# Two norms with their sums on all rows, and a sigmoid made of exponential and reciprocal, in a two-block transformer kernel

## What is computed

```python
def rms_norm(x, g):
    xf = x.astype(jnp.float32)
    y = xf * lax.rsqrt(jnp.mean(xf * xf, axis=-1, keepdims=True) + EPS)
    return (y * g.astype(jnp.float32)).astype(x.dtype)
...
        h = h + rms_norm(mixed, norm_gains[layer, 1])
        ...
        h = h + rms_norm(ffn, norm_gains[layer, 3])
    return h[:, N_META:]
...
    h = h * norm_g.astype(jnp.float32).reshape(MLSTM_HEADS, MLSTM_HEAD_DIM)
    h = h.reshape(B, S, MLSTM_WIDTH) * jax.nn.sigmoid(o_pre.astype(jnp.float32))
```

## Time and profile before

| | |
|---|---|
| median of 3 runs | 1566.23 us (1563.57 to 1566.26) |
| profiled execution | 1566.23 us, its span 1564.4 us |
| TensorE busy | 1520.0 us, 97% of the span |
| VectorE busy | 1025.5 us, 66% |
| ScalarE busy | 655.5 us, 42% |
| GpSimd busy | 21.9 us, 1% |
| DMA | 147.61 MB, mean 94 GB/s |

### The profile page before, as it was taken

The page is one execution under the profiler, slowest core; times in us unless marked ns, Lnnn a source line. Parts: engine busy times, 40 slices in busy tenths (PEclk is TensorE's granted clock), DMA queues, the critical chain, the costliest instruction groups (busy, mean ns, idle before and its releaser), DMA issues. The chain is left out here.

```text
span 1564.4 us, 25875 instructions
## 1 busy us (share of the span) xinstructions
PE 1520.0 (97%) x10760; PEld 1351.7 (86%) x10760; DVE 1025.5 (66%) x1441; ACT 655.5 (42%) x1052; POOL 21.9 (1%) x20
## 2 busy tenths in 40 slices
PE   7999999999998999999999899999999999999998
PEld 7988878888998999999888677767677999998876
DVE  5533445785446887777656666676687888885453
ACT  5433442433334222122343545545645555554343
POOL 0000000000000000000000002000000000000000
PEclk9999999999999999999999999999999999999999
DMA  5221104452331233232445213110013232222322
GB/s 180 82 82 58 38 15 155 136 165 88 106 108 68 102 129 107 102 135 75 135 134 176 94 48 102 61 35 28 28 54 108 81 109 107 97 97 83 95 90 81
DMA packets 37699, 147.61 MB, mean 94 GB/s; under 512 B 4304, under 2 KB 4432, under 8 KB 27856
## 3 DMA queue, kind: packets, MB, share of 16 engines
q1 hardware_dynamic: 36288, 142.76, 27.6%
q10 hardware_dynamic: 1152, 2.16, 0.4%
q0 software_dynamic: 144, 1.05, 0.2%
HBM read 143.86 MB, written 2.10 MB: 93 GB/s over the span
## 5 line engine op out<-in xcount | busy, mean ns | idle before, releaser
L567 PE MATMUL ps<-t 128*128 128x258 f32 (+4 forms) x2160 | 689.6, 319 | 23.7 <-DVE t L2298 8.7
L569 PE MATMUL ps<-t 128*128 128x258 f32 (+4 forms) x2160 | 678.3, 314 | 0.0
L568 PE MATMUL ps<-t 128*128 128x258 f32 (+4 forms) x2160 | 677.4, 314 | 0.0
L567 PEld LDWEIGHTS ps<-t 128*128 128x128 f32 (+1 forms) x2160 | 408.8, 189 | 67.7 <-issue 16.9
L569 PEld LDWEIGHTS ps<-t 128*128 128x128 f32 (+1 forms) x2160 | 408.5, 189 | 27.1
L568 PEld LDWEIGHTS ps<-t 128*128 128x128 f32 (+1 forms) x2160 | 409.4, 190 | 23.7
L2250 DVE TENSOR_TENSOR t<-t 128x1024 fp32r<-128x1024 f32 (+2 forms) x121 | 205.8, 1700 | 204.9 <-ACT t L1525 204.9
L1525 ACT ACTIVATE t<-t 128x1024 fp32r<-128x1024 f32 (+2 forms) x121 | 174.0, 1438 | 187.0 <-PE ps L569 175.0
L1474 PE MATMUL ps<-t 128*128 128x256 f32 x504 | 142.6, 283 | 0.0
L1472 PE MATMUL ps<-t 128*128 128x256 f32 x504 | 142.5, 283 | 0.1
L1473 PE MATMUL ps<-t 128*128 128x256 f32 x504 | 141.3, 280 | 0.0
(11 more groups left out here) (328 smaller groups left out, 1832.4 us busy)
## 6 DMA issues: line engine op xcount, KB each, us to landing
t<-in_W SPq DMA_DIRECT2D x75, 1024.0 KB, 4.8
t<-in_W SPq DMA_DIRECT2D x62, 512.0 KB, 3.6
t<-in_W SPq DMA_DIRECT2D x100, 256.0 KB, 3.8
t<-in_W SPq DMA_DIRECT2D x4, 644.0 KB, 3.8
t<-in_XT ACTq DMA_DIRECT2D x8, 264.0 KB, 7.7
out<-t SPq DMA_DIRECT2D x8, 256.0 KB, 2.5
t<-in_ROPE POOLq DMA_DIRECT2D x1, 1024.0 KB, 5.3
t<-in_CONS SPq DMA_DIRECT2D x1, 423.0 KB, 11.2
```

The lines of the kernel that those rows point to most:

```text
L567: pe.matmul(out, wh, xh, start=first, stop=False)
L568: pe.matmul(out, wh, xl, start=False, stop=False)
L569: return pe.matmul(out, wl, xh, start=False, stop=last)
```

## The change

Three things are changed.

1. Norms 1 and 3 sum over the rows by products whose left side is all ones (over 1024) on 128 rows and columns, and whose right side is the squares themselves, 512 columns wide (and 4 more for norm 1). The sums then stand on all 128 rows at once. The root is taken from there into `rst`, the reciprocal by VectorE in `rst`, and `norm_spread` and `spread` are gone for these two.
2. The gate tiles are evacuated as exp(-x), and VectorE adds 1 and takes the reciprocal, one tile at the end of each of the units 3 to 6, in place of a plain evacuation, the tanh in unit 15 and the scalings in unit 16.
3. Semaphore counts follow (`pow` and `spr` go up by two where a norm's turn was dropped).

```diff
+            def norm_total(i, b):
+
+                n, ones = NORM_N[i], C("o1024").to_broadcast([P, P])
+                for src, last in ((norm_acc(i), False), (sq[1][:, 0:n], True)):
+                    if last:
+                        pe.wait_ge(S["sq"], 8 * i + 8)
+                    else:
+                        pe.wait_ge(S["sum"], SUM0[i + 1])
+                    ins = pe.matmul(bank(b, 512), ones, src[:, 0:512], start=not last, stop=last)
+                    if n > 512:
+                        ins = pe.matmul(bank(b + 1, n - 512), ones, src[:, 512:n], start=not last, stop=last)
+                    ins.then_inc(S["col"], 1)
...
-            norm_sums(1, 4)
-            norm_sum_of(1, 4, 7)
-            norm_spread(1, 4)
+            norm_total(1, 4)
...
-            norm_sums(3, 0)
-            norm_sum_of(3, 0, 7)
-            norm_spread(3, 0)
+            norm_total(3, 0)
...
             def root(i, b):
-                ac.activation(rcol[:, 0:nc_], bank(b, nc_), ACT.Sqrt, bias=con[:, a:z]).then_inc(S["eps"], 1)
+                ac.activation(rst[:, 0:NORM_N[i]], bank(b, NORM_N[i]), ACT.Sqrt, bias=con[:, a:z]).then_inc(S["eps"], 1)
...
             root(1, 4)
-            spread(1, 4)
...
             root(3, 0)
-            spread(3, 0)
...
-            dv.reciprocal(rcol[:, 0:5], rcol[:, 0:5]).then_inc(S["pow"], 1)
+            dv.reciprocal(rst[:, 0:TQ], rst[:, 0:TQ]).then_inc(S["rst"], 1)
...
-            dv.reciprocal(rcol[:, 0:4], rcol[:, 0:4]).then_inc(S["pow"], 1)
+            dv.reciprocal(rst[:, 0:T2], rst[:, 0:T2]).then_inc(S["rst"], 1)
...
-                    ac.activation(sig[:, f - 1, :], bank(f % 2, T2), ACT.Copy).then_inc(S["ev_o2"], 1)
+                    ac.activation(sig[:, f - 1, :], bank(f % 2, T2), ACT.Exp, scale=-1.0).then_inc(S["ev_o2"], 1)
...
-                    for k in range(4):
-                        ac.wait_ge(S["ev_o2"], k + 1)
-                        ac.activation(sig[:, k, :], sig[:, k, :], ACT.Tanh, scale=0.5).then_inc(S["o2_s"], 1)
...
-                    dv.wait_ge(S["o2_s"], 4)
-                    for k in range(4):
-                        dv.tensor_scalar(sig[:, k, :], sig[:, k, :], 0.5, 0.5, ALU.mult, ALU.add).then_inc(S["o2_s"], 1)
...
+                if 3 <= u <= 6:
+                    e = sig[:, u - 3, :]
+                    dv.wait_ge(S["ev_o2"], u - 2)
+                    dv.tensor_scalar(e, e, 1.0, None, ALU.add).then_inc(S["o2_s"], 1)
+                    dv.wait_ge(S["o2_s"], 2 * u - 5)
+                    dv.reciprocal(e, e).then_inc(S["o2_s"], 1)
```

More of the change, by code:

```diff
@@ L535, in rstd @@
                 po.tensor_tensor(rcol[:, 0:n], rcol[:, 0:n], half[:, 0:n], ALU.pow
-                                 ).then_inc(S["pow"], 1)
+                                 ).then_inc(S["pow"], 2 if i in (2, 4) else 1)
             po.memset(half[:, :], -0.5).then_inc(S["half"], 1)
@@ L628, in norm_sum_of @@
                 col_stat(sq[k % 2][:, 0:n], n, b, k == 0, C("o1024")[:, 0:1], off).then_inc(S["col"], 1)
+            def norm_total(i, b):
[9 more added lines that the diff above has]
+                    ins.then_inc(S["col"], 1)
             def norm_spread(i, b):
                 pe.wait_ge(S["pow"], i + 1)
-                col_spread(b, NORM_N[i], rcol).then_inc(S["spr"], 1)
+                col_spread(b, NORM_N[i], rcol).then_inc(S["spr"], 2 if i == 4 else 1)
             def spread_aside(n):
@@ L979, in _ @@
             pe.wait_ge(S["ev_wo_d"], 4)
-            pe.wait_ge(S["rst"], 2)
+            pe.wait_ge(S["eps"], 2)
             for k in range(8):
@@ L1001, in _ @@
                     pe.wait_ge(S["pow"], 3)
-                    spread_aside(TQ).then_inc(S["spr"], 1)
+                    spread_aside(TQ).then_inc(S["spr"], 2)
             ins.then_inc(S["mm_up"], 1)
@@ L1071, in _ @@
             shift_rows(0, w)
-            pe.wait_ge(S["rst"], 4)
+            pe.wait_ge(S["eps"], 4)
             pe.wait_ge(S["ev_dn_d"], 4)
@@ L1558, in root @@
                 a, z = CON["eps"]
-                nc_ = (NORM_N[i] + 127) // 128
                 ac.wait_ge(S["col"], COL0[i + 1])
-                ac.activation(rcol[:, 0:nc_], bank(b, nc_), ACT.Sqrt, bias=con[:, a:z]).then_inc(S["eps"], 1)
+                ac.activation(rst[:, 0:NORM_N[i]], bank(b, NORM_N[i]), ACT.Sqrt, bias=con[:, a:z]).then_inc(S["eps"], 1)
             def spread(i, b):
```

## The result

| | before | changed | ratio, 95% interval |
|---|---|---|---|
| median of 4 runs | 1565.18 us | 1576.76 us | 1.0076 [1.0058, 1.0093] |
| range of the runs | 1563.57 to 1566.26 | 1575.83 to 1578.11 | |

The profiled execution of the changed kernel is not one of the four in the table; it took 1580.75 us, 4 us above their median. Part of that has nothing to do with the change: by 142 us, ahead of every changed instruction, it is already 1.9 us behind the profiled execution of before.

A forecast was written before the change was run, and what follows sets the result against it. The prediction took TensorE, busy in 97% of the span, as the bound. Its terms, 2.7 + 0.3 + 1.9 + 0.5 + 17.0 + 0 = 22.4, added to 1566.23 gave 1588.6 us, range 1579 to 1598.

The forecast's parts named there:

- the price of the wide reciprocal: VectorE, six reciprocals of 512 or 516 columns: 8.3 ns for each column, so 4.4 us for 512.
- The clock terms: TensorE at half clock behind the longer waits at the norms: 0.3 us added at norm 1, 0.5 at norm 3.
- The forecast's steps in the attention: Units 3 to 6: each addition and reciprocal delays VectorE's next row maximum by 4.9 us; 17.0 of 19.6 us reach TensorE.
- four waits named: TensorE waits for ScalarE's copy of the turned tile in units 4 to 7: 2.6, 3.2, 6 and 3 us.
- Norms: First scaling on VectorE behind the wide root and reciprocal: 2.7 us later at norm 1, 1.9 at norm 3.
- (a): Rival, VectorE: a wide reciprocal runs at the ordinary rate, 0.7 us; 1566.5 us, no change; 6%.
- (b): Rival, attention: VectorE's idle time ahead of its splits swallows the reciprocals, only the norms count; 1571.6 us; 6%.
- (c): Rival, attention: TensorE's clock stays low through two whole units behind the new waits, 8 us in all; 1596.6 us; 10%.
- (d): Rival, VectorE: the steepest price of the reciprocal, 6.3 us for 512 columns; 1600 us; 4%.
- What goes: ScalarE's four tanh (2.18 us) and VectorE's four scalings dropped: wins nothing, 0.7 us at most.

The follow-up runs named there:

- widths test: Kernel before with reciprocals of 1 to 512 columns, and additions, added behind VectorE's last instruction; one execution, 1569.25 us.
- the kernel with that copy ahead: Against the sigmoid alone: in units 4 to 7 ScalarE copies the turned tile ahead of the exponentials; 1577.29 us, ratio 1.0072.
- cheap-reciprocal kernel: Changed kernel with its six wide reciprocals replaced by a multiplication by 1 of the same width; 1561.59 us, ratio 0.9973.
- air kernel: Against the sigmoid alone: additions and reciprocals moved behind the row maximum, ahead of the split, in units 3, 5, 7, 9; 1564.65 us, ratio 0.9991.
- the sigmoid alone: Changed kernel with norms 1 and 3 turned back to those of before, the gate as changed; 1576.77 us, ratio 1.0081.
- norms alone: Changed kernel with the gate's sigmoid turned back to that of before, norms 1 and 3 as changed; 1565.95 us, ratio 1.0004.
- logarithm: Against norms alone: wide root and VectorE's reciprocal replaced by a logarithm and exp(-x/2) on ScalarE; 1560.68 us, ratio 0.9977.
- both: Kernel before with the norms by logarithm and exponential, and the gate's reciprocals as in the air kernel; 1559.91 us, ratio 0.9963.

## Why the forecast had the direction and missed the size

**The step that failed** is the price of the wide reciprocal: "From two columns to five that is (191 - 166)/3 = 8.3 ns for each column". Measured, it is 6.25, and 3.35 us in place of 4.4. The 25 ns of difference between two small durations were read as three columns' price, and the widths test shows that such durations move by some 10 ns without any reason in the width (164 for one column, 155 for two, 191 and 181 for five). The kernel before had shown it too. Beside line 2368 it has sixteen more reciprocals of two columns, which the forecast didn't use (VectorE by source line, as in the earlier trace rows):

```profile
L2741 DVE RECIPROCAL t<-t x16: 96/159/166, 954.8 to 1088.0; 128x2 f32<-128x2 f32 x16
```

Their median is 159 ns where that of line 2368 is 166, and one of them took 96. With 159 the same slope would be (191 - 159)/3 = 10.7. Ten ns on three columns are 3.3 ns a column, multiplied by 510. "Four widths lie on that line within 5 ns" was no support: from 166 at two columns a slope of 6.25 gives 178.5 at four and 185 at five, where 179 and 191 stand. The range that these rows allow is 8.3 with 3.3 to either side, 5 to 11.6 ns; it holds 6.25, but the forecast priced nothing between 0.5 us and 4.4.

The price alone doesn't account for the whole distance. Between the forecast's 1588.6 and the measured 1576.76 lie 11.8 us. With 3.35 for 4.4 and everything else as it was put, the sum is 1.6 + 0.3 + 0.9 + 0.5 + 12.7 = 16.0, so the price is 6.4 of them. The clock terms are 2.3 (0.8 was put in, 1.5 came back), the start from 1566.23 where the four executions have 1565.18 is 1.1, and 2.1 are the distance from 13.7 (the steps with the measured price and clock, summed below) to the 11.6 of the medians, which is within their interval. The lower end of the range, 1579, was worked out from no price: at 5 ns a column, 2.7 us for a reciprocal, the forecast's own steps give 12.1 and 1578.3, by an estimate.

The forecast had set a sentence of the Trainium skill beside its slope (VectorE: DVE Perf Modes, the walkthrough of the 8-slice pipeline: a repeat count of 8), from which an estimate of 8.3 ns a column comes out; that both gave 8.3 supported neither. By the 0.96 GHz in the specifications of the same page of the Trainium skill, the measured 6.25 ns are 6 cycles and not 8, and the measurement decides.

**The rest of the steps, with 3.35 for 4.4.** The new work of a unit is 3.85 instead of 4.9. The forecast's steps in the attention, carried through with that, against the turns measured (start in the changed kernel minus start in the earlier trace rows, less the 2.86 that it brought along). The two turns of before that the earlier trace rows doesn't show:

```profile
1009.50 0.60 PE L1162 MATMUL ps<-t 128*128 128x128 f32 x4
1018.45 0.60 PE L1162 MATMUL ps<-t 128*128 128x128 f32 x4
```

| turn before | forecast | with 3.85 | measured |
|---|---|---|---|
| 1000.55 | 2.6 | 1.5 | 4.24 - 2.86 = 1.4 |
| 1009.50 | 5.8 | 3.6 | 6.40 - 2.86 = 3.5 |
| 1018.45 | 12.2 | 9.0 | 11.52 - 2.86 = 8.7 |
| 1027.40 | 15.2 | 10.9 | 13.23 - 2.86 = 10.4 |
| 1032.40 | 17.0 | 12.7 | 14.88 - 2.86 = 12.0 |

So the lateness of the row maximum, the dense VectorE row from unit 4 on and the missing recovery behind it all held, and ScalarE's copy is the wait by which it mostly reached TensorE, though not the only one by which it can, as the kernel with that copy ahead shows; four unit costs of 3.85 are 15.4, and 12.3 of them reach the end. Of the four waits named, three came (1.25, 1.97 and 3.40 for ScalarE's copy, where 2.6, 3.2 and 6 were forecast at the price of 4.4); the one in unit 7 didn't, and stands at the next turn, 1.97 for VectorE's copy. They add up to 8.6 us, less than the 12.0 of the last row, since TensorE partly waits and partly works at half clock: the mean clock of 0.94 over the 60 us of 985 to 1045 is, by an estimate, 3.6 us of work.

**Norms.** Scaling at norm 1 forecast 2.7 later, measured 1.6; with 3.38 for 4.4 it is 480.95 + 0.04 + 3.38 + 0.05 = 484.4 against 482.84, 1.6. Norm 3 by the same 0.9 for 1.9. The two clock terms, +0.3 and +0.5, were the second thing that was mis-sized: behind norm 3 TensorE did wait over 5 us (5.5) and its clock did fall, as forecast, but VectorE's offset stayed at 2.86, and behind norm 1 there was a gain of 1.5.
In sum 1.6 - 1.5 + 0.9 + 12.7 = 13.7 by the forecast's own steps with the measured price and clock, 13.3 in the profiles, 11.6 in the medians.

**Rivals.** (a) fell with the duration: a wide reciprocal is no ordinary operation. The cheap-reciprocal kernel has its price, and shows that the case would have been worth -3.3 and not the 0.3 it was given. (b), that the attention swallows the reciprocals, is false where they were put and true in another place of the same units. (c) TensorE does run at half clock behind the new waits, but for some 3 us and not through whole units: the mean granted clock of 985 to 1045 us is 0.94. It took air only: the table's middle column has no clock term, and the measured one is no larger. (The stretch behind the wait of 3.40, changed kernel:)

```profile
1030.00:1033.00 3.00, 3.00 (x10) 1.32 (x11) 2.93 (x6) 1.21 (x2) 0.00 (x0) 0.64 0.00 0
1033.00:1036.00 3.00, 3.00 (x12) 2.37 (x11) 3.00 (x2) 0.00 (x0) 0.00 (x0) 0.79 0.00 0
```

(d), the steepest price, is out with the measured 3.35.

**What goes** (tanh and scalings): worth nothing, as forecast; in the air kernel their absence moved the time by -0.2.

## What to carry to other kernels

Don't scale a slope from a few columns to a few hundred: put the scatter of one such duration through the same factor, and keep that as the range of the price, with the time worked out at both of its ends. An expensive instruction on an engine with a third of its time idle costs nothing or most of its length (here 11.9 of 15.4 us) by where it stands in the row: put it behind the operation that others wait for, where its engine would wait anyway, and not ahead of it. A reciprocal over a wide tile costs seven times an ordinary operation here (3.35 us for 512 columns against 0.49); if a logarithm and an exponential are at hand on ScalarE, the inverse root costs 0.63 us more than the root.

## What the runs showed that was not expected

The clock behind norm 1. In the kernel before, TensorE's granted clock falls a second time some 20 us behind the norm, behind twenty records of one-column products (those of the next norm). Timeline of TensorE, before:

```profile
507.49 2.29 PE L610 MATMUL ps<-t 128*128 128x1 f32 x20
509.64 0.53 PE L567 MATMUL ps<-t 128*128 128x258 f32 x1
509.96 0.42 PE L568 MATMUL ps<-t 128*128 128x258 f32 x1
```

The same place in the changed kernel:

```profile
510.98 2.29 PE L610 MATMUL ps<-t 128*128 128x1 f32 x20
513.13 0.36 PE L567 MATMUL ps<-t 128*128 128x258 f32 x1
513.33 0.28 PE L568 MATMUL ps<-t 128*128 128x258 f32 x1
```

The one-column products take the same 2.29 us in both; behind them a product takes 0.42 us (half clock, 1.2 GHz) in the one and 0.28 (full) in the other. The windows of the two stretches, before and then changed:

```profile
509.00:512.00 3.00, 3.00 (x18) 3.00 (x19) 2.28 (x2) 0.27 (x1) 1.84 (x1) 0.62 0.00 0
```

```profile
512.00:515.00 3.00, 3.00 (x27) 3.00 (x27) 2.37 (x2) 0.63 (x2) 1.29 (x1) 1.00 0.00 0
```

That is the 1.5 us: VectorE's offset is 3.46 ahead of these products and 1.98 behind them. The second fall is there, at or within a microsecond or two of that place, in each of the five profiles whose norm 1 has one-column sums and a spread (before, the sigmoid alone, in the air, ScalarE's copy ahead, the widths), and in none of the five with wide sums (changed, norms alone, cheap, logarithm, both). The wait ahead of norm 1's first tile differs among the five: 7.4 us in the norms alone, 4.7 with the logarithm, against 3.85 before. So neither the reciprocal nor the length of the wait decides it. What in the history does, the kind of products at the norm or the moment at which they stand, was not separated by a run; it is open.

Besides, the profiled executions differ by several microseconds ahead of 142 us where no instruction differs, and half-clock stretches come in one execution and not in another. The changed kernel's, 120 to 130 us (before has the clock at 1.00 there):

```profile
120.00:130.00 10.00, 10.00 (x83) 8.79 (x82) 2.15 (x6) 1.90 (x7) 0.00 (x0) 0.83 0.14 56
```

Norm 1 has such scatter too: in the widths kernel, whose code there is that of before, it came 1.0 us later than in the profile of before, at a clock that fell earlier. So a difference of a microsecond or so between two single profiles shows nothing by itself. The differences above were taken as steps, and the times as medians.
